# A fused two-layer encoder trunk: the wait ahead of the first attention head, the order of ScalarE's weight roundings in the heads, and the order of the tail behind them

## The reference

```
h    = rms_norm(x); proj = h @ w_in              # 1024 -> 3616: conv 1024, c_q 256, c_kv 256, k_rope 32, gates 2048
conv = silu(layer_norm(depthwise31(a * sigmoid(g)))) @ w_conv_out
q    = rope(rms_norm(rms_norm(c_q)  @ w_uq))     # 8 heads of 96
k, v = from rms_norm(c_kv) @ w_ukv and k_rope;  k = rope(rms_norm(k))
o    = softmax(q k^T / sqrt(96), chunk-causal mask) v;  mla = o @ w_mla_out
x    = x + (sigmoid(gate0) * conv + sigmoid(gate1) * mla) @ w_out
```

## Time and profile before

| | |
|---|---|
| median of 3 runs | 1125.14 us (1124.57 to 1125.21) |
| profiled execution: time, span | 1121.82 us, 1120.0 us |
| mean granted clock of PE | 0.991 |
| busy share PE, PEld, DVE, ACT, POOL | 97%, 81%, 59%, 46%, 19% |
| mean DMA rate | 176 GB/s |
| mixer of layer 0 | about 205 to 375 us of the span |
| mixer of layer 1 | 553.4 us later, with the same pattern |

### The profile page before, as it was taken

How to read it: one execution, slowest core, us unless ns; L and a number is a source line. 1 busy time by engine, 2 the same in 40 slices (tenths; PEclk the granted TensorE clock), 3 DMA queues, 4 the chain that set the end, 5 groups by cost and what they waited for, 6 DMA issues and landing times.

```text
span 1120.0 us, 14519 instructions
## 1 busy us (share of the span) xinstructions
PE 1089.3 (97%) x5323; PEld 906.9 (81%) x5328; DVE 661.9 (59%) x854; ACT 511.3 (46%) x642; POOL 210.8 (19%) x252
## 2 busy tenths in 40 slices
PE   8999999997999999999999999999889999999998
PEld 5888888896888888888868888889878888888886
DVE  4654555588976555545365544556899665545443
ACT  5443444565563344434254344336655625444441
POOL 3810000148630000000057000002576100000000
PEclk9999999998999999999999999999989999999999
DMA  7856556355445175465446555554464443565550
GB/s 243 263 163 213 187 165 238 107 197 194 161 141 188 48 248 187 156 220 188 135 147 229 187 177 197 209 184 158 154 212 154 132 150 118 195 213 187 163 175 38
DMA packets 134477, 196.66 MB, mean 176 GB/s; under 512 B 6944, under 2 KB 105504, under 8 KB 134432
## 3 DMA queue, kind: packets, MB, share of 16 engines
q1 hardware_dynamic: 132560, 192.39, 51.9%
q10 hardware_dynamic: 1872, 3.67, 1.1%
HBM read 194.98 MB, written 1.05 MB: 175 GB/s over the span
## 4 chain that ended last, share of the span: by engine, by line
PE 87%; DVE 7%; DMA 2%; ACT 1%; issue 1%; POOL 1%; SPq 0%; ACTq 0%; DVEq 0%
PE bank L546 27%; PE bank L548 27%; PE bank L547 27%; DVE wlo L1179 3%; PE bank L611 2%; DVE bank L1289 1%; DMA raw<-in_w_in 1%; POOL small L421 1%; DMA raw<-in_ffn_w_up 1%; PE bank L702 1%; DVE small L1368 1%; ACT whi L917 1%; PE bank L714 1%; DVE small L1348 1%; PE bank L576 1%
## 5 line engine op out<-in xcount | busy, mean ns | idle before, releaser
L1179 DVE TENSOR_TENSOR wlo<-raw,whi 128x2048 fp32r<-128x2048 f32 (+2 forms) x160 | 362.2, 2287 | 119.6 <-ACT whi L917 119.5
L546 PE MATMUL bank<-whi,hThi 128*128 128x512 f32 (+1 forms) x992 | 392.3, 395 | 6.1 <-DVE hTlo L1184 4.7
L548 PE MATMUL bank<-whi,hTlo 128*128 128x512 f32 (+1 forms) x992 | 382.2, 385 | 0.0
L547 PE MATMUL bank<-wlo,hThi 128*128 128x512 f32 (+1 forms) x992 | 382.1, 385 | 0.0
L917 ACT ACTIVATE whi<-raw 128x2048 fp32r<-128x2048 f32 (+1 forms) x180 | 339.4, 1909 | 29.6 <-DMA raw<-in_ffn_w_up 12.0
L546 PEld LDWEIGHTS bank<-whi,hThi 128*128 128x128 f32 x992 | 187.7, 189 | 44.6 <-DVE hTlo L1184 6.3
L548 PEld LDWEIGHTS bank<-whi,hTlo 128*128 128x128 f32 x992 | 187.5, 189 | 37.3
L547 PEld LDWEIGHTS bank<-wlo,hThi 128*128 128x128 f32 x992 | 187.8, 189 | 34.1
L546 PE MATMUL bank<-whi,gThi 128*128 128x512 f32 (+1 forms) x416 | 165.0, 397 | 0.0
L941 ACT ACTIVATE gates<-bank 128x256 f32<-128x256 f32 x88 | 33.8, 384 | 281.7 <-PE bank L548 281.7
L548 PE MATMUL bank<-whi,gTlo 128*128 128x512 f32 (+1 forms) x416 | 161.6, 388 | 0.0
(11 more groups left out here) (146 smaller groups left out, 775.2 us busy)
## 6 DMA issues: line engine op xcount, KB each, us to landing
raw<-in_ffn_w_gate SPq DMA_DIRECT2D x88, 512.0 KB, 4.0
raw<-in_ffn_w_up SPq DMA_DIRECT2D x88, 512.0 KB, 5.2
raw<-in_ffn_w_down SPq DMA_DIRECT2D x88, 512.0 KB, 4.1
raw<-in_w_in SPq DMA_DIRECT2D x48, 512.0 KB, 4.8
raw<-in_w_out SPq DMA_DIRECT2D x16, 512.0 KB, 4.1
raw<-in_w_in SPq DMA_DIRECT2D x8, 544.0 KB, 4.6
raw<-in_w_mla_out SPq DMA_DIRECT2D x8, 512.0 KB, 4.1
raw<-in_w_conv_out SPq DMA_DIRECT2D x8, 512.0 KB, 4.0
```

Of the source, the lines that this page charges most:

```text
L546: nc.tensor.matmul(out, lh, rh, start=start, stop=False, skip_group_check=skip)
L547: nc.tensor.matmul(out, lh, rl, start=False, stop=False, skip_group_check=skip)
L548: return nc.tensor.matmul(out, ll, rh, start=False, stop=stop, skip_group_check=skip)
L1179: nc.vector.tensor_tensor(wlo[:, slot(u0, RING), 0:n], raw[:, slot(u0, RAW), 0:n], whi[:, slot(u0, RING), 0:n].bitcast(F32), ALU.subtract) ...
```

## The change

- PE's turn of head 0 waits for `qk_norm` once, the keys' multiply, instead of twice. The queries' factor is made on POOL, a `tensor_tensor` of 16 columns by a constant, right behind the two roots, with a semaphore of its own that DVE's first `head_max` waits for.
- DVE: the remainder of UM+9, which stood ahead of the keys' multiply, is made behind it, and that of UM+10 behind the second `conv_gate`; eight taps take the former place. L1368 is gone. Ahead of `head_max(0)` stand 4 taps instead of 14, behind it 10.
- ACT: the roundings of UM+12 and UM+13, which stood ahead of head 0, move to units 1 and 2; all that follow are one or two places later, and units 3 and 5 take a second one behind the exponentials.
- PE: the transposes of the second norm half go in after 36 of the 48 matmuls of the projection's first half.
- PE's tail: values of head 6 and transposes of the probabilities of head 7 go in after 6 of the 12 matmuls of unit 7, t = 1; values of head 7, mean and the transposes of the output after 9 of them. The variance goes between the two units of `w_mla_out` for t = 0, `root_rows` ahead of those for t = 1. ACT rounds the output's rows ahead of squaring for the variance. DVE makes their remainders ahead of the last gate bias.
- Silu, rounding and remainder of the convolution's rows go in two halves, each with its semaphore; DVE's remainder of UM+21 moves from in front of the first gated sum to behind these.

```
--- before.py
+++ after.py
@@ -70,7 +70,7 @@
-EARLY_TAPS = (10, 8)
+EARLY_TAPS = (10, 8, 8)
 POOL_FIRST, POOL_LAST = UM + 11, UM + 20
@@ -160,6 +160,7 @@
         neg_max = small[:, 80:82]
+        neg_scale = small[:, 93:94]
         psum_h = small[:, 82:84]
@@ -228,6 +229,7 @@
         qk_norm = sem("qk_norm")
+        qscale_ready = sem("qscale_ready")
         pool_step = sem("pool_step")
@@ -413,7 +415,8 @@
             nc.gpsimd.memset(mean_of[:, :], 1.0 / C).then_inc(const_ready, 1)
-            pool.wait_ge(const_ready, 3)
+            nc.gpsimd.memset(neg_scale, -SCALE).then_inc(const_ready, 1)
+            pool.wait_ge(const_ready, 4)
             nc.gpsimd.affine_select(out=ident[:, :], in_=ident[:, :], compare_op=ALU.not_equal, fill=1.0,
@@ -524,6 +527,9 @@
                 root(rsqk[:, 0:16], ssqk[:, 0:16]).then_inc(qk_rs, 1)
+                pool.wait_ge(qk_rs, (l + 1) * 2)
+                nc.gpsimd.tensor_tensor(neg_qscale, rsqk[:, 0:16], neg_scale.to_broadcast([P, 16]),
+                                        ALU.mult).then_inc(qscale_ready, 1)
                 unit_waits(pool, l, POOL_FIRST - 1)
@@ -693,7 +699,7 @@
                     pe.wait_ge(pool_step, (l + 1) * N_ROT)
-                    pe.wait_ge(qk_norm, (l + 1) * 2)
+                    pe.wait_ge(qk_norm, l + 1)
                 else:
@@ -764,14 +770,16 @@
             def mixer(l):
-                for t in range(TT):
-                    norm(l, 1, t)
+                norm(l, 1, 0)
+                for t in range(TT):
                     for h in range(2):
                         for k in range(4):
+                            if (t, h, k) == (0, 1, 2):
+                                norm(l, 1, 1)
                             for m in range(2):
@@ -807,6 +815,16 @@
                 conv_in(l, 1, M_C23, 0)
+
+                def out_turn():
+
+                    for t in range(TT):
+                        if t == 0:
+                            pe.wait_ge(o_ready, (l + 1) * H)
+                        for k in range(4):
+                            ins = nc.tensor.transpose(bank[:, 4 + t, k * P:(k + 1) * P],
+                                                      otok[:, t, k * P:(k + 1) * P], ident[:, :])
+                        ins.then_inc(ot_done, 1)
                 for u8 in range(8):
@@ -827,6 +845,13 @@
                         for k in range(4):
+                            if (u8, t, k) == (H - 1, 1, 2):
+                                head_values(l, H - 2)
+                                head_probs(l, H - 1)
+                            if (u8, t, k) == (H - 1, 1, 3):
+                                head_values(l, H - 1)
+                                mean(l)
+                                out_turn()
                             ins = products(bank[:, b0 + t, :], hT(4 * kh + k, t), wt(u, 2048, 4, k, slice(0, 512)),
@@ -837,21 +862,11 @@
                         if t == 1:
-                            if u8:
+                            if u8 == 0:
+                                head_scores(l, 0)
+                            elif u8 < H - 1:
                                 head_values(l, u8 - 1)
-                            else:
-                                head_scores(l, 0)
-                head_probs(l, H - 1)
-                mean(l)
-                head_values(l, H - 1)
-
-                for t in range(TT):
-                    if t == 0:
-                        pe.wait_ge(o_ready, (l + 1) * H)
-                    for k in range(4):
-                        ins = nc.tensor.transpose(bank[:, 4 + t, k * P:(k + 1) * P], otok[:, t, k * P:(k + 1) * P],
-                                                  ident[:, :])
-                    ins.then_inc(ot_done, 1)
+
                 def variance():
@@ -867,15 +882,19 @@
                                      stop=True).then_inc(lnb_done, 1)
-                variance()
-
-                pe.wait_ge(xc_ready, l + 1)
                 for t in range(TT):
                     pe.wait_ge(ot_lo, l * 2 + t + 1)
+                    if t == 0:
+                        pe.wait_ge(xc_ready, l + 1)
                     pe.wait_ge(gate_sum, l * 8 + (6 if t == 0 else 8))
-                    rows_out(l, UM + M_MLA, 2, hT, t, 2 - 2 * t, mla_done, between={1: root_rows} if t == 0 else {})
-                pe.wait_ge(c_lo, l + 1)
+                    rows_out(l, UM + M_MLA, 2, hT, t, 2 - 2 * t, mla_done,
+                             between={1: variance} if t == 0 else {0: root_rows})
+
+                def conv_half(h):
+
+                    pe.wait_ge(c_lo, l * 2 + h + 1)
+
                 def y_turn(t):
@@ -886,7 +905,8 @@
                         ins.then_inc(yt_done, 1)
-                rows_out(l, UM + M_CO, 2, gT, 0, 4, co_done)
+                rows_out(l, UM + M_CO, 2, gT, 0, 4, co_done,
+                         between={0: lambda: conv_half(0), 1: lambda: conv_half(1)})
                 rows_out(l, UM + M_CO, 2, gT, 1, 6, co_done, between={1: lambda: y_turn(0)})
@@ -895,7 +915,7 @@
             pe.sem_inc(unit_free, RING)
-            pe.wait_ge(const_ready, 4)
+            pe.wait_ge(const_ready, 5)
             pe.wait_ge(dve_const, 1)
@@ -1071,7 +1091,6 @@
                 one()
-                one()
                 def head_copy(h):
@@ -1115,26 +1133,30 @@
                     head_exp(u8)
+                    if u8 in (3, 5):
+                        one()
                 head_probs(H - 1)
-                act.wait_ge(xc_ready, l + 1)
-                nc.scalar.activation(csq, cacc[:, :, :], ACT.Square).then_inc(csq_ready, 1)
                 for t in range(TT):
                                          ACT.Copy).then_inc(ot_hi, 1)
+                act.wait_ge(xc_ready, l + 1)
+                nc.scalar.activation(csq, cacc[:, :, :], ACT.Square).then_inc(csq_ready, 1)
                 gate_tanh(3)
                 act.wait_ge(ln_ready, l + 1)
-                for ct in range(CT):
-                    nc.scalar.activation(cacc[:, ct, :], cacc[:, ct, :], ACT.Silu,
-                                         scale=vec[:, V_LG + ct:V_LG + ct + 1],
-                                         bias=vec[:, V_LB + ct:V_LB + ct + 1]).then_inc(act_silu, 1)
-                act.wait_ge(act_silu, (l + 1) * CT)
-                nc.scalar.activation(gThi[:, :, :], cacc[:, :, :], ACT.Copy).then_inc(c_hi, 1)
+                for h in range(2):
+                    for ct in (2 * h, 2 * h + 1):
+                        nc.scalar.activation(cacc[:, ct, :], cacc[:, ct, :], ACT.Silu,
+                                             scale=vec[:, V_LG + ct:V_LG + ct + 1],
+                                             bias=vec[:, V_LB + ct:V_LB + ct + 1]).then_inc(act_silu, 1)
+                    act.wait_ge(act_silu, l * CT + 2 * h + 2)
+                    nc.scalar.activation(gThi[:, 2 * h:2 * h + 2, :], cacc[:, 2 * h:2 * h + 2, :],
+                                         ACT.Copy).then_inc(c_hi, 1)
                 one()
@@ -1353,7 +1375,7 @@
                 sums(1)
-                one()
+                taps(EARLY_TAPS[2])
                 dve.wait_ge(qk_rs, l * 2 + 1)
@@ -1361,12 +1383,10 @@
                 conv_gate(1, 0)
+                one()
                 assert next(s) == POOL_FIRST
                     next(s)
-                dve.wait_ge(qk_rs, l * 2 + 2)
-                nc.vector.tensor_scalar(neg_qscale, rsqk[:, 0:16], -SCALE, None, ALU.mult).then_inc(qk_norm, 1)
-
                 def head_max(h):
@@ -1374,7 +1394,7 @@
                     if h == 0:
-                        dve.wait_ge(qk_norm, (l + 1) * 2)
+                        dve.wait_ge(qscale_ready, l + 1)
                     nc.vector.memset(small[:, 94:95], 0.0)
@@ -1405,8 +1425,9 @@
                                                 bias[:, :], ALU.add).then_inc(gate_sum, 1)
-                taps(14)
+                taps(4)
                 head_max(0)
+                taps(10)
                 for u8 in range(1, 8):
@@ -1419,17 +1440,17 @@
                 head_sum(H - 1)
+                head_out(H - 1)
                 dve.wait_ge(mean_done, l + 1)
                                         ALU.subtract).then_inc(xc_ready, 1)
-                head_out(H - 1)
-                gate_bias(3)
                 for t in range(TT):
                          hThi[:, 0:4, t * P:(t + 1) * P]).then_inc(ot_lo, 1)
+                gate_bias(3)
                 assert done[0] == N_TAP
@@ -1449,13 +1470,15 @@
                                         ALU.mult).then_inc(ln_ready, 1)
-                unit_waits(dve, l, POOL_LAST)
-                one()
                 dve.wait_ge(gate_ready, (l + 1) * 8)
                 gated(0, 1, 2, ym_ready)
-                dve.wait_ge(c_hi, l + 1)
-                rest(gTlo[:, :, :], cacc[:, :, :], gThi[:, :, :]).then_inc(c_lo, 1)
+                for h in range(2):
+                    dve.wait_ge(c_hi, l * 2 + h + 1)
```

(4 more changed lines are left out.)

## The result

The changed kernel takes 1111.71 us (median, 1111.54 to 1112.11) against 1124.97 before (four executions; the 1125.14 of the forecast was the median of three): ratio 0.9883, 95% interval 0.9866 to 0.9900, 13.3 us faster. Forecast were 1115.3 and 9.8 us, range 1110.5 to 1119.8. The two profiled executions differ by less: 1111.56 us with a span of 1109.8 against 1121.82 and 1120.0, 10.3 us, where the sum said 9.8.

A forecast was written before the change was run, and what follows sets the result against it. PE, busy 97% of the span, was taken to bound the kernel. Per layer 0.6 + 6.0 + 0.3 - 2.0 = 4.9 us, 9.8 for two, took the median from 1125.14 to 1115.3 us; range 1110.5 to 1119.8.

The forecast's parts named there:

- The norm half: Input projection, transposes of the second norm half: gap of 0.98 us shrinks to 0.3, gain 0.6 us a layer.
- Ahead of the heads: Up to the first maximum: keys' root 2.9 us instead of 4.86, no PE wait at head 0's turn, `head_max(0)` at 259.8.
- its bounds: GpSimd's factor of 16 columns ahead of the heads: 0.25 us below, 2.2 above if a remainder holds it off.
- Heads 0 to 7: New PE gaps of 1.5 and 1.7 us, DVE gives back 3.2 of 9.2; head 7's scores 5.9 to 6.0 earlier.
- the 17 taps: DVE's 10 + 7 taps between two maxima, instead of 7, 0.39 us each; PE waits 1.5 us at head 0's values.
- The tail: Behind head 7: 0.90 us gap becomes 0.3; DVE's late remainder of UM+21 makes PE give back 2.0 us at merged rows.
- Sum: Whole kernel: 4.9 us a layer, 9.8 for two; profiled execution 1121.8 to 1112.0 us, median 1125.14 to 1115.3.
- rival (a): Tail doesn't stall, `y_turn(0)` meets its rows: gain 6.9 us a layer, 1111.3 us; chance 0.12.
- Rival (c): New gaps of 1.5, 1.7 and 2.0 us a layer each bring a half-clock spell, 2.9 us each: 1132.7; chance 0.06.
- (b): Keys' factor late, root stays 4.86 us or queries' root holds the multiply: gain 2.2 to 3.1 a layer, 1119.5; chance 0.15.

The follow-up runs named there:

- Experiment 2: Kernel before with only the queries' factor on POOL, L1368 gone and PE's single wait: 1124.73 us, ratio 1.0003.
- experiment 3: Kernel before with the queries' factor on GpSimd, PE's single wait and ACT's new order in the heads: 1114.65 us, ratio 0.9910.
- Experiment 9: Changed kernel with 3 taps behind the first maximum instead of 10: 1106.64 us; with 14 taps: 1115.80 us.
- Experiment 8: Changed kernel with rounding and remainder of UM+21 moved forward, ahead of the last gate tanh and the wait for the variance: 1108.27 us.
- experiment 1: Kernel before, unchanged, in 12 executions: 1124.77 us, ratio 0.9999.
- experiment 6: Kernel before with only the new order of PE, ACT and DVE from the last head to the output products: 1124.13 us, ratio 0.9998.
- experiment 5: Changed kernel with the old order of PE, ACT and DVE from the last head to the output products: 1110.00 us.
- experiment 4: Changed kernel with the remainder of UM+9 ahead of the keys' multiply again, the eight taps behind the second conv_gate: 1117.41 us.

## Why the prediction was right, and what it missed

**The norm half.** The gap became 0.20 us, forecast 0.3. In the profile PE reaches the turn of head 0 at 254.77, 0.9 ahead of 255.7; forecast 0.6. Taken back it costs 2.0 us for both layers, 1.0 each (0.9 and 0.8 in the profile): the term was 0.2 to 0.4 too small.

**Ahead of the heads.** Each step came: the wait is gone, both roots take 2.9 us, the multiply isn't held by the second root although it starts 0.08 us behind it (249.88, 1.75 us long). By this case's rows the rule of the Trainium skill ("SBUF — State Buffer", "Who interferes with whom") that whichever starts first has the shared port pair for its whole length doesn't reach these two instructions. For DVE's remainder against POOL's root and factor the rows agree with it. The factor took 1.12 us, inside its bounds, and nobody waited for it. That ACT's order is a condition for the gain was not said: the prediction costed ACT's moves at nothing, having checked only that nothing comes too late. It used the free ACT (copy at once behind the turn) without naming what freed it. Experiment 2 shows that taking the wait at the turn away alone is worth 0.0 us, experiment 3 that ACT's order makes it worth 10.0.

**Heads 0 to 7.** Gaps of 1.45 and 1.31 us, forecast 1.5 and 1.7, each behind the DVE instruction named. The maximum of head 7 stands at 311.89 instead of 318.75, 6.9 earlier; forecast 6.0 and 0.6. Between the first maximum and the last DVE gives back 3.1 us (53.06 against 49.95), forecast 3.2. Experiment 9 shows the 17 taps to be the cause of both gaps.

**The tail.** The wait ahead of `w_mla_out` was 0.34 us, forecast 0.3, and the merged rows' gap 1.44 us, forecast 1.6; PE is through the transposes 5.2 us earlier than in the earlier trace rows (343.8 against 349.0), forecast 4.3 and 0.6. Experiment 8 shows the remainder of UM+21 to be what makes it.

**Sum.** Profiled against profiled: 10.3 us, forecast 9.8. What failed is the last step, "it lay 3.3 below the median, so the median goes from 1125.14 to 1115.3". That carried the 3.3 us over as if they were constant. They are half-clock spells of PE behind the heads (experiment 1), which the profiled execution happened not to have and which no profile with the new tail shows (experiments 1 and 6); the changed kernel's median and profile are 0.2 apart. That the median still lies inside the range is in part luck: the low end was set by rival (a), which didn't come about. The forecast thus missed a gain of the change: its tail was read as a loss of 1.7 us a layer, which it is in an execution at full clock (1.7 us for both layers in experiment 5, plus 1.6 for the spell in it), and not in the common one (experiment 6). The mean clock of 0.991 was in the table; that its distance to the median might be clock was not asked. Rival (c) even held that gaps of 0.9 to 1.0 us can hardly have lowered anything; in experiment 1 the clock does fall behind such a gap and the small matmuls after it. A mean clock alone doesn't place a spell either: part of that 0.991 is one at 10 to 16 us of the span (0.72, where the changed kernel has 1.00), and the mixer of layer 0 begins at the same time with it (204.97 us) and without it (205.01).

**The rivals.** (a) has the measured time but not its mechanism: the gap at the merged rows is there. (b) is out by the rows above: the root takes 2.9 us and the multiply isn't held; experiment 4 shows what a held root costs. (c) didn't occur at 1.3 to 1.5 us: three of four executions had a mean clock of 1.000, the fourth 0.998. It does occur behind the gaps of 2.5 to 3.1 us, in both layers of both profiled executions that have them (experiments 3 and 9), and behind 2.11 us in one of two layers (experiment 4). But its price of 2.9 us a spell, which makes up its 1132.7, is too high for the two gaps in the heads: where DVE set the pace, a spell cost nothing (experiments 4 and 9).

Not settled: what in the old tail decides whether the clock falls in a given execution, and which part of the new order keeps it up, since that takes away the 0.90 us gap and breaks up the run of small matmuls at once.

## What to carry to other kernels

A wait taken away is worth what the next wait in line allows: look at what every other engine does between the two, a weight's rounding that waits for a DMA included. Before summing, ask why the profiled execution is faster than the median; if the mean clock is below 1, the difference may be a cost that the profile doesn't show, and a change may remove it. A spell of half clock costs nothing where another engine sets the pace, so price it by the stage in which it falls. And when an instruction of 16 columns takes microseconds, look at what VectorE or GpSimd is doing beside it.

## What the runs showed of the hardware

- DVE's tensor-scalar of 16 columns stood 3.98 us, to the end of a GpSimd subtraction; GpSimd's root of 16 columns took 4.9 us instead of 2.9 beside a DVE subtraction with two SBUF inputs, and 2.9 beside taps that read one input from PSUM. A DVE multiply of two SBUF operands (1.75 us) that began 0.08 us behind a GpSimd root was not held.
- PE's clock fell to 1.2 GHz without a gap above 0.9 us, behind that gap and a stretch of transposes and one-column matmuls (0.66 and 0.61 over 5 us, experiment 1), and stayed at 2.4 in another execution of the same program.
- The kernel before scatters by 5 us (1121.1 to 1126.3), with the new tail alone by 3 us (1122.2 to 1125.2, twelve executions), the changed kernel by 0.6 us (1111.5 to 1112.1, four).
- Half-clock spells in the heads (0.72 over 6 us in both layers with 14 taps, 0.50 over 2 us in layer 0 of experiment 4) left the time from first to last maximum as it was.
